# Mixers: the scores of two differential heads in four row groups at once, the values of two latent heads in two column groups at once

## The reference

```
z = rmsnorm(h) @ w_in           # split: c_q, c_kv, k_rope, dq, dk, dv, p_in, gates
# latent mixer, 8 heads: scores over 96 dimensions (64 + 32 with rotation), values of 64
p = softmax(mask((qn @ kn.T + qr @ kr.T) * scale));  o_mla[h] = p @ v[h]
# differential mixer, 8 heads of two maps m = 0, 1, each over 32 dimensions, values of 64
p[m] = softmax(mask(q[h, m] @ k[h, m].T * scale - slope[h] * dist))
o_diff[h] = (p[0] - lam * p[1]) @ v[h]
# pool mixer: causal averages over windows of 2, 4, 8, 16, then a 128x128 product per group
h = h + (sum over branches of sigmoid(gate) * (branch @ w_branch)) @ w_out
```

## Time and profile before

| | before |
|---|---|
| median of three runs | 1540.04 us (1538.98 to 1542.37) |
| profiled execution | 1535.66 us |
| its span, first to last instruction | 1533.9 us |
| granted TensorE clock, mean | 1.000 |
| TensorE busy | 1520.0 us (99%) |
| VectorE busy | 1188.6 us (77%) |
| ScalarE busy | 803.2 us (52%) |
| GpSimd busy | 44.5 us (3%) |

### The profile page before, as it was taken

How to read it: one execution, slowest core, us unless ns; L and a number is a source line. 1 busy time by engine, 2 the same in 40 slices (tenths; PEclk the granted TensorE clock), 3 DMA queues, 4 the chain that set the end, 5 groups by cost and what they waited for, 6 DMA issues and landing times.

```text
span 1533.9 us, 26661 instructions
## 1 busy us (share of the span) xinstructions
PE 1520.0 (99%) x11410; PEld 1428.5 (93%) x11410; DVE 1188.6 (77%) x1579; ACT 803.2 (52%) x1030; POOL 44.5 (3%) x43
## 2 busy tenths in 40 slices
PE   7999999999999999999999999999999999999999
PEld 6999999999999999899999999999999999999989
DVE  7787788788887777976778778779998898666844
ACT  6444455565454445544455455455545745775654
POOL 0000010210000000000001110000000000000000
PEclk9999999999999999999999999999999999999999
DMA  7555444334455555555544433456554453325531
GB/s 279 209 190 185 175 152 184 138 125 144 174 194 189 186 185 190 192 192 182 190 152 168 157 138 138 152 189 236 176 203 175 165 192 115 135 85 191 181 135 56
DMA packets 38693, 260.59 MB, mean 170 GB/s; under 512 B 4656, under 2 KB 5040, under 8 KB 9136
## 3 DMA queue, kind: packets, MB, share of 16 engines
q1 hardware_dynamic: 37856, 257.84, 47.3%
q10 hardware_dynamic: 720, 1.05, 0.2%
HBM read 257.83 MB, written 1.05 MB: 169 GB/s over the span
## 4 chain that ended last, share of the span: by engine, by line
PE 95%; DVE 3%; ACT 1%; DMA 0%; issue 0%; ACTq 0%
PE ps L255 21%; PE ps L204 19%; PE ps L206 18%; PE ps L205 18%; PE ps L257 11%; DVE w_low L194 1%; PE ps L1253 1%; ACT w_high L187 1%; PE ps L1265 1%; PE ps L2054 1%; PE ps L2037 0%; PE ps L1245 0%; PE ps L1238 0%; PE ps L1237 0%; DMA w_raw<-in_weights 0%; PE ps L2479 0%
## 5 line engine op out<-in xcount | busy, mean ns | idle before, releaser
L187 ACT ACTIVATE w_high<-w_raw 128x2048 fp32r<-128x2048 f32 (+3 forms) x244 | 458.8, 1882 | 494.7 <-PE ps L206 271.2
L194 DVE TENSOR_TENSOR w_low<-w_raw,w_high 128x2048 fp32r<-128x2048 f32 (+3 forms) x244 | 552.1, 2264 | 116.6 <-ACT w_high L187 114.8
L255 PE MATMUL ps<-x,w_high 128*128 128x512 f32 x1408 | 495.3, 395 | 9.3 <-DVE w_low L698 9.3
L257 PE MATMUL ps<-x,w_low 128*128 128x256 f32 x1408 | 395.5, 281 | 0.0
L255 PEld LDWEIGHTS ps<-x,w_high 128*128 128x128 f32 x1408 | 264.8, 188 | 67.5 <-issue 9.3
L257 PEld LDWEIGHTS ps<-x,w_low 128*128 128x128 f32 x1408 | 267.3, 190 | 0.1
L204 PE MATMUL ps<-x,w_high 128*128 128x256 f32 (+1 forms) x904 | 261.7, 289 | 0.2 <-DVE x L291 0.2
L206 PE MATMUL ps<-x,w_low 128*128 128x256 f32 (+1 forms) x904 | 255.9, 283 | 0.0
L205 PE MATMUL ps<-x,w_high 128*128 128x256 f32 (+1 forms) x904 | 255.8, 283 | 0.0
L204 PE MATMUL ps<-ffn_hid_high,w_high 128*128 128x256 f32 x704 | 197.8, 281 | 0.0
L205 PE MATMUL ps<-ffn_hid_low,w_high 128*128 128x256 f32 x704 | 197.2, 280 | 0.0
(11 more groups left out here) (439 smaller groups left out, 2322.3 us busy)
## 6 DMA issues: line engine op xcount, KB each, us to landing
w_raw<-in_weights SPq DMA_DIRECT2D x229, 1024.0 KB, 4.8
w_raw<-in_weights SPq DMA_DIRECT2D x10, 768.0 KB, 4.2
w_raw<-in_weights SPq DMA_DIRECT2D x5, 512.0 KB, 3.9
even_second_vectors<-in_second SPq DMA_DIRECT2D x1, 1836.0 KB, 7.1
w_raw<-in_weights SPq DMA_DIRECT2D x2, 640.0 KB, 3.9
resid<-in_x SPq DMA_DIRECT2D x4, 256.0 KB, 5.9
w_raw<-in_weights ACTq DMA_DIRECT2D x4, 256.0 KB, 7.7
out<-resid SPq DMA_DIRECT2D x3, 256.0 KB, 2.5
```

Of the source, the lines that this page charges most:

```text
L187: act.activation(self.wh[:, j, 0:SIZES[n]], self.raw[:, j, 0:SIZES[n]], ACT.Copy).then_inc(self.hi_made, 1)
L194: dve.tensor_tensor(self.wl[:, j, 0:SIZES[n]], self.raw[:, j, 0:SIZES[n]], self.wh[:, j, 0:SIZES[n]].bitcast(F32), ALU.subtract).then_inc( ...
L255: pe.matmul(c.bank(bank + i).rearrange("p (a t) -> p a t", a=2), wh[:, k, f], c.x[:, :, k, :], start=(k == 0), stop=False, skip_group_chec ...
L257: mm = pe.matmul(c.bank(bank + i, SEQ), wl[:, k, f], c.xh[:, k, :], start=False, stop=(k == DT - 1), skip_group_check=True)
```

## The change

- The scores of the differential heads 2i and 2i + 1 are made together in the step of the even one (`pair_scores`): eight matmuls in four row groups, the 128-column ones of all four groups first, then the 256-column ones; each group has its own bank, 2 to 5. The odd step has no scores. `read_scores` finds them in banks 2 and 3 or 4 and 5.
- The values of the latent heads 2p and 2p + 1 are made together in step 2p + 3 (`pair_values`), in two column groups of bank 7, tile by tile, the two heads in turn. ScalarE and VectorE read all 128 partitions once for a pair. Steps 2, 4, 6 and 8 have no values.
- Banks: scores 2 to 5, turned probabilities 6 alone (so `turn(a)` waits for the copy of turn a - 1, before for that of a - 2), values 7, pooling products 4 and 5. Projection units from S_DK to the last gate slot use banks 0 and 1 in turn and wait for unit u - 2; all others keep u % 3 and u - 3.

```diff
--- before.py
+++ after.py
@@ -740,7 +740,7 @@
 
 BRANCH_ORDER = (0, 2, 1)
 GATE_ORDER = (2, 0, 1)
-B_S, B_T, B_O = 3, 5, 7
+B_S, B_POOL, B_T, B_O = 2, 4, 6, 7
 
 
 UNITS = ([(n, 0, "dve") for n in range(S_UQ)] + [(S_UQ, p, "act") for p in range(4)]
@@ -754,6 +754,21 @@
     return next(u for u, x in enumerate(UNITS) if x[:2] == (n, part))
 
 
+FIRST_PAIRED, FIRST_BRANCH = unit_of(S_DK), unit_of(S_BRANCH)
+
+
+def unit_bank(u):
+
+
+    return u % 2 if FIRST_PAIRED <= u < FIRST_BRANCH else u % 3
+
+
+def bank_user(u):
+
+
+    return u - 2 if FIRST_PAIRED <= u < FIRST_BRANCH else u - 3
+
+
 def emptied(u):
 
     return sum(x[2] == UNITS[u][2] for x in UNITS[:u + 1])
@@ -762,8 +777,8 @@
 MIX_SEMS = dict(
     read_a=emptied(unit_of(S_POOL - 1)), read_d=emptied(unit_of(S_OUT - 1, 1)), latent_sq=2, latent_sum=1, latent_rt=1,
     latent_n=3, latent_hi=2, latent_lo=2, latent_diag=1, latent_wide=1, krope_in=1, krope_done=1, q_roped=4, k_spread=1,
-    scored=16, scores_read=16, max_made=16, exped=16, probs_made=16, turned=16, turned_copied=16, pv_done=16, o_high=8,
-    o_read=16, bias_made=8, lam_sum=1, lam_exp=1, lam_made=2, pool_zero=3, pool_step=4, pool_avg=4, pool_w=1, pool_y=4,
+    scored=16, scores_read=16, max_made=16, exped=16, probs_made=16, turned=16, turned_copied=16, pv_done=16, o_high=4,
+    o_read=12, bias_made=8, lam_sum=1, lam_exp=1, lam_made=2, pool_zero=3, pool_step=4, pool_avg=4, pool_w=1, pool_y=4,
     pool_h=1, pool_l=1, gated=12, d_sq=1, d_ms=1, d_rt=1, d_n=1, d_t=1, d_y=2, d_h=1, d_l=1, merged=8, merged_high=4,
     merged_low=4)
 
@@ -853,7 +868,7 @@
 
         def evac(u):
             n, part, _ = UNITS[u]
-            bank = u % 3
+            bank = unit_bank(u)
             act.wait_ge(*self.filled(u))
             if n == S_UQ:
                 ins = act.activation(m.q[0:QK, 2 * part:2 * part + 2, :], c.halves(bank)[0:QK], ACT.Copy)
@@ -890,12 +905,11 @@
             act.wait_ge(*t["turned"](a + 1))
             if a >= 2:
                 act.wait_ge(*t["pv_done"](a - 1))
-            act.activation(m.pt[:, a % 2, :], c.bank(B_T + a % 2, 3 * P), ACT.Copy).then_inc(t["turned_copied"].sem, 1)
-
-        def out_high(a):
-            act.wait_ge(*t["pv_done"](a + 1))
-            r = slice(64 * (a % 2), 64 * (a % 2) + 64)
-            act.activation(m.yh[r, a // 2, :], c.bank(B_O, SEQ)[r, :], ACT.Copy).then_inc(t["o_high"].sem, 1)
+            act.activation(m.pt[:, a % 2, :], c.bank(B_T, 3 * P), ACT.Copy).then_inc(t["turned_copied"].sem, 1)
+
+        def out_high(p):
+            act.wait_ge(*t["pv_done"](2 * p + 2))
+            act.activation(m.yh[:, p, :], c.bank(B_O, SEQ), ACT.Copy).then_inc(t["o_high"].sem, 1)
 
         after(S_CQ)
         self.norm.root(act)
@@ -929,8 +943,8 @@
                 copy_turned(a - 1)
             if a < 2 * HEADS:
                 exps(a)
-            if 2 <= a < HEADS + 2:
-                out_high(a - 2)
+            if 2 <= a < HEADS + 2 and a % 2:
+                out_high((a - 2) // 2)
             if n >= S_GATE:
                 tanh(n)
 
@@ -944,7 +958,7 @@
 
         for n in range(S_BRANCH, S_OUT):
             if n == S_BRANCH:
-                act.wait_ge(*t["o_read"](2 * HEADS))
+                act.wait_ge(*t["o_read"](HEADS // 2 + HEADS))
                 act.activation(m.dq[:, :, :].rearrange("p a t -> p (a t)"),
                                od[:, :, :, :].rearrange("p a h d -> p (a h d)"), ACT.Square).then_inc(t["d_sq"].sem, 1)
             if n < S_OUT - 1:
@@ -990,7 +1004,7 @@
 
         def evac(n):
             u = unit_of(n)
-            ps = c.halves(u % 3)
+            ps = c.halves(unit_bank(u))
             dve.wait_ge(*self.filled(u))
             if n == S_CKV:
                 dve.tensor_tensor(m.kr[rows, :], ps[rows, 1, :], c.rstd[rows, 0:SEQ], ALU.mult).then_inc(t["krope_in"].sem, 1)
@@ -1026,7 +1040,7 @@
             if diff:
                 dve.wait_ge(*t["bias_made"](a - HEADS + 1))
             for x in range(1 + diff):
-                bank = B_S + (x if diff else a % 2)
+                bank = B_S + (2 * (a % 2) + x if diff else a % 2)
                 for j, cols in enumerate((slice(0, P), slice(P, 3 * P))):
                     add = m.bias[:, a % 2, cols] if diff else c.tab[:, T_CAUSAL + cols.start:T_CAUSAL + cols.stop]
                     i = 2 * x + j
@@ -1060,9 +1074,11 @@
 
         def take_out(a):
             if a < HEADS:
-                r = slice(64 * (a % 2), 64 * (a % 2) + 64)
-                dve.wait_ge(*t["o_high"](a + 1))
-                dve.tensor_tensor(m.yl[r, a // 2, :], c.bank(B_O, SEQ)[r, :], m.yh[r, a // 2, :].bitcast(F32),
+                if a % 2 == 0:
+                    return
+                p = a // 2
+                dve.wait_ge(*t["o_high"](p + 1))
+                dve.tensor_tensor(m.yl[:, p, :], c.bank(B_O, SEQ), m.yh[:, p, :].bitcast(F32),
                                   ALU.subtract).then_inc(t["o_read"].sem, 1)
             else:
                 dve.wait_ge(*t["pv_done"](a + 1))
@@ -1136,7 +1152,7 @@
             if a == 2 * HEADS:
                 dve.wait_ge(*t["pool_w"](1))
                 for g in range(4):
-                    dve.tensor_scalar(m.pp[:, g, PAD:], c.halves(B_S + g // 2)[:, g % 2, :], V[:, V_PB + g:V_PB + g + 1],
+                    dve.tensor_scalar(m.pp[:, g, PAD:], c.halves(B_POOL + g // 2)[:, g % 2, :], V[:, V_PB + g:V_PB + g + 1],
                                       V[:, V_PS + g:V_PS + g + 1], ALU.add, ALU.mult).then_inc(t["pool_y"].sem, 1)
         dve.wait_ge(*t["pool_h"](1))
         dve.tensor_tensor(m.pl[:, :, :], m.pp[:, :, PAD:], m.ph[:, :, :].bitcast(F32), ALU.subtract).then_inc(t["pool_l"].sem, 1)
@@ -1160,7 +1176,7 @@
                 g = gates[b][:, 4 * half + 2 * part:4 * half + 2 * part + 2, :]
                 x = m.q[:, 4 * half + 2 * part:4 * half + 2 * part + 2, :]
                 dve.wait_ge(*self.filled(u))
-                dve.scalar_tensor_tensor(out=g, in0=g, scalar=1.0, in1=c.halves(u % 3), op0=ALU.add,
+                dve.scalar_tensor_tensor(out=g, in0=g, scalar=1.0, in1=c.halves(unit_bank(u)), op0=ALU.add,
                                          op1=ALU.mult).then_inc(t["read_d"].sem, 1)
                 if b:
                     dve.wait_ge(*t["read_d"](emptied(u)))
@@ -1184,7 +1200,7 @@
             u, b = unit_of(n), n - S_OUT
             h = c.h[:, 2 * b:2 * b + 2, :]
             dve.wait_ge(*self.filled(u))
-            dve.scalar_tensor_tensor(out=h, in0=c.halves(u % 3), scalar=0.5, in1=h, op0=ALU.mult,
+            dve.scalar_tensor_tensor(out=h, in0=c.halves(unit_bank(u)), scalar=0.5, in1=h, op0=ALU.mult,
                                      op1=ALU.add).then_inc(c.resid_done, 1)
             if b < 3:
                 after(n)
@@ -1202,9 +1218,10 @@
 
         def bank_free(u):
             if u >= 3:
-                pe.wait_ge(*t["read_a" if UNITS[u - 3][2] == "act" else "read_d"](emptied(u - 3)) if UNITS[u - 3][2] != "resid"
-                           else self.resid(emptied(u - 3) - 1))
-            return u % 3
+                v = bank_user(u)
+                kind = UNITS[v][2]
+                pe.wait_ge(*(self.resid(emptied(v) - 1) if kind == "resid" else t["read_a" if kind == "act" else "read_d"](emptied(v))))
+            return unit_bank(u)
 
         def plain(n, norm=None, midway=None):
 
@@ -1227,49 +1244,62 @@
             mm.then_inc(c.done, 1)
 
         def scores(a):
-            h = a % HEADS
-            if a >= HEADS:
-                pe.wait_ge(*t["scores_read"](a))
-                for x in range(2):
-                    g = 2 * (h % 2) + x
+            h = a
+            if a >= 2:
+                pe.wait_ge(*t["scores_read"](a - 1))
+            pe.wait_ge(*t["q_roped"](h // 2 + 1))
+            o = c.bank(B_S + a % 2)
+            pe.matmul(o[:, 0:P], m.q[0:QK, h, 0:P], m.k[0:QK, h, 0:P], start=True, stop=True)
+            pe.matmul(o[:, P:3 * P], m.q[0:QK, h, P:SEQ], m.k[0:QK, h, :], start=True,
+                      stop=True).then_inc(t["scored"].sem, 1)
+
+        def pair_scores(a):
+
+
+            pe.wait_ge(*t["scores_read"](a))
+            pair = (a - HEADS) // 2
+            for q, o, k in ((slice(0, P), slice(0, P), slice(0, P)), (slice(P, SEQ), slice(P, 3 * P), slice(0, SEQ))):
+                for g in range(4):
                     r = slice(DH * g, DH * g + DH)
-                    o = c.bank(B_S + x)
-                    pe.matmul(o[:, 0:P], m.dq[r, h // 2, 0:P], m.dk[r, h // 2, 0:P], start=True, stop=True)
-                    mm = pe.matmul(o[:, P:3 * P], m.dq[r, h // 2, P:SEQ], m.dk[r, h // 2, :], start=True, stop=True)
-            else:
-                if a >= 2:
-                    pe.wait_ge(*t["scores_read"](a - 1))
-                pe.wait_ge(*t["q_roped"](h // 2 + 1))
-                o = c.bank(B_S + a % 2)
-                pe.matmul(o[:, 0:P], m.q[0:QK, h, 0:P], m.k[0:QK, h, 0:P], start=True, stop=True)
```

(60 more changed lines are left out.)

## The result

| | before | after |
|---|---|---|
| median | 1539.62 us (1538.98 to 1542.37, 4 runs) | 1526.14 us (1521.95 to 1527.03, 4 runs) |
| ratio | | 0.9904, 95% interval 0.9882 to 0.9926 |
| profiled execution | 1535.66 us | 1527.03 us |
| its span | 1533.9 us | 1525.3 us |

13.5 us less, forecast 13.7. The interval of the ratio spans 11.4 to 18.2 us, so these runs alone do not fix the gain more closely.

What follows compares the result with a forecast made beforehand. TensorE, busy 99% of the span, was taken as the bound. 3.96 + 3.03 + 0.19 - 0.25 - 0.10 = 6.83 us a layer, 13.7 us in two, gave 1526.3 us from the median 1540.04; range 1521.5 to 1534.

Steps and rivals of the forecast that it cites:

- Latent values: Steps 2, 4, 6 and 8 lose their values, 0.99 us each, 3.96 us a layer; the second head nearly free.
- Differential scores: Steps 9, 11 and 13 lose 1.01 us each, 3.03 a layer; second pair of groups costs 0.01, bounds 0 and 0.66.
- Step 15 gives its gain back: Missing scores bring 0.19 us, not 1.01; TensorE idles some 0.9 us before step 16's pooling matmuls, waiting for VectorE's averages.
- The first bank: First S_DK projection unit waits for ScalarE's read of the first latent V part; 0.25 us a layer lost, restart included.
- One bank for the turned probabilities: A turn waits for the copy of the last one, one step old; claimed to cost nothing.
- VectorE's cover: VectorE needs 6.73 us in a step with differential scores, a step without lasts 6.75; it fits, barely.
- rival 3: VectorE bounds short steps 9, 11, 13, 15: 0.2 us of room, half a us more costs 4 us, 1530.3 us; chance 0.10.
- Rival 1: In a pair's scores, row groups go two at a time: 0.66 us a pair, 5.3 in all, 1531.6 us; chance 0.09.
- Rival 2: Neither scores nor values pair; heads run one behind the other inside a visit: 1536.9 us; chance 0.03.
- Rival 5: Four row groups run together but a stream takes longer: 0.2 us a pair, 1.6 us, 1527.9 us; chance 0.05.
- Rival 6: New idle time before the pooling matmuls brings TensorE's clock down; 1549 us with four half-clock projections; chance 0.03.
- Rival 4: No wait ahead of the pooling, as VectorE reaches its averages earlier: 8 tenths of a us a layer back, 1524.7; chance 0.06.

Runs made afterwards that it cites:

- the order test: Changed kernel with a pair's eight score matmuls written row group after row group, not all 128-column ones first; 1526.14 us.
- the test with six operations: Changed kernel with six more VectorE operations at the end of each of steps 9, 11 and 13; 1533.22 us.
- the version without the two waits: Changed kernel with pool averages spread over steps 8, 10, 12, 14 and the loop's first projection unit left in bank 2; 1523.67 us, 0.9901 of the kernel before.

## Why the prediction was right, by its steps

- **TensorE as the bound: right.** What left its stream left the loop, to 0.02 us in steps where nobody else waits.
- **Latent values, 3.96 us a layer: right** (3.95 with the pairing alone, the extra 0.01 us a pair included).
- **Differential scores, 1.01 us a step: right** (7.76 to 6.75). The claim that two groups overlapped already, so that one visit in two is the gain, is shown by the order test. For four groups at once, which no row of before showed, the prediction chose the lower end of its two bounds, 0.01 us, and that was the step with the least under it; measured are 0.87 us against 0.86. By the Trainium skill's 3.07 for four row groups ("TensorE: Matmul & The Clock Gate", "Part 3: Packing small matmuls"; a measurement with 512 columns), read as the pace of the stream, a pair would have taken 0.2 us more, an estimate. Here it did not, in the pair's visit or with the stream doubled; the measurement decides.
- **Step 15 gives its gain back: right.** Forecast 0.19 us kept of 1.01 and TensorE idle for 0.9; measured 16.23 us for steps 15 and 16 (347.24 to 363.47) against 16.41, so 0.18 kept, and 0.79 us idle. Moving the averages brought 1.00 us back, the lost 0.83 and the 0.16 that TensorE had idled there before (361.49 to 361.65), which shows that they were the cause.
- **The first bank, 0.25 us a layer: right** (0.27; the restart cost 0.11 and not 0.08), and shown by the bank left where it was. No later bank wait appeared.
- **One bank for the turned probabilities: right.** No wait on the copies is listed.
- **The sum** was 6.83 us a layer: 7.10 off the loop less 0.27 at its start is 6.83. (Its last term, eight pairs with 0.01 us more, is 0.08 and not 0.10; the range as described comes to 1521.1 and 1534.7 us, not 1521.5 and 1534.) This agreement, loop against loop, is that of the mechanism. That the medians, too, agree to 0.2 us is closer than their scatter allows, and so in part luck. For the profiled execution 1522.0 us were forecast and 1527.03 came, because the profiled execution of the kernel before was the quick one; the pace of the feed-forward stages is what the prediction took for a constant.
- **VectorE's cover: the step that was wrong.** "It fits, barely", and rival 3's price, counted VectorE's idle time in a short step as all its room and every further 0.1 us as TensorE's wait. With 0.88 us more the loop did not move. What TensorE waits for is the probabilities at the next turn. In the changed kernel's timeline those of the long step 10 are ready at 316.52 + 0.75 = 317.27 and the turn comes at 318.32, those of the short step 11 at 324.03 + 0.75 = 324.78 and 326.03, and a delay is first taken up by the idle time of both steps: 1.5 to 1.8 us a pair, as the test with six operations shows, and not 0.2. In steps 9, 11 and 13 the 0.5 us of rival 3 would have cost nothing; only step 15, where the pooling matmuls wait for VectorE, has no such room. The forecast did not rest on that price, but the rival's chance did.
- **Rivals 1, 2, 5 and 6** are excluded by the starts and the length of the visits and by the granted clock. Rival 4 did not come true.

## What to carry to other kernels

Where TensorE is the bound, small matmuls in separate row or column groups cost one stream and one visit however many groups they fill (seen here with four row groups and with two column groups), so gather work of the same shape from two steps into one visit, and price the gain as visits spared (here 0.65 us of stream and 0.36 of switching), not by the number of groups: groups written one behind the other may run together already. When a step gets shorter, look for the one step in which another engine's chain ends just in time, and move its optional work (here the pool averages) into steps that stayed long. The room of a covering engine is its idle time over the whole period in which its lateness can be made up (here a long and a short step), looked at from the point where its result is used, and not its idle time in the step that got shorter.

## What the runs showed of the hardware

TensorE starts matmuls of other row groups ahead of written order: with the 256-column matmul of each group ahead of the next group's first, four groups still started within 0.05 us.

The same kernel has executions of two paces in the feed-forward stages. The groups of instructions of L255 (the 512-column matmuls; busy us, mean ns), of the two profiles of the kernel before:

```profile
L255 PE MATMUL ps<-x,w_high 128*128 128x512 f32 x1408 | 495.3, 395 | 9.3 <-DVE w_low L698 9.3
```

```profile
L255 PE MATMUL ps<-x,w_high 128*128 128x512 f32 x1408 | 499.6, 398 | 9.5 <-DVE w_low L698 9.4
```

At a granted clock of 1.000 in both, the stretch shown above takes 470.5 or 474.5 us. Of the eleven other profiles of this study one more was quick there (the version without the two waits), so that its span of 1518.5 us must not be compared with the changed kernel's 1524.7. The mean of L255's matmuls tells the two paces apart: 395 and 396 ns in the two quick profiles, 398 to 400 in the other eleven of the thirteen. What decides the pace of an execution stays open; it was not tried.
